# The first mixer of a two-block transformer in another order: latents and values first, attention beside the forget gates, recurrence beside gates and half of the output projection

## The chip, the cores and the metric

One core of a Trainium2 chip runs the whole kernel. The metric is the device time of one execution in microseconds; the time given is the median of three runs. The engines are TensorE (PE in the profile), VectorE (DVE), ScalarE (ACT), GpSimd (POOL) and SyncE (SP), which issues nearly all transfers here.

## What is computed

Two transformer blocks on 256 tokens of width 2048, all in float32. Only the first mixer concerns the change:

```python
mod = (cond @ w_mod[layer] + b_mod[layer])            # six sections of 2048, cond = silu(c)
shift_a, scale_a, gate_a, shift_m, scale_m, gate_m = split(mod)
h = _rmsnorm(x, pre_mix_g[layer]) * (1.0 + scale_a) + shift_a
proj = h @ w_in[layer]                                # 512 + 256 + 64 + 5 * 1024 columns
q_lat, kv_lat, k_rope, hq, f_fwd, f_bwd, hi, hg = jnp.split(proj, offsets, axis=-1)
attn_out = _mla(...)      # rmsnorm of latents, w_uq, w_ukv, rotation, 8 heads, softmax, values
rec_out = _hgrn2_bidir(...)   # two gated recurrences (f_fwd, f_bwd) over values hi, norm, silu(hg)
mix = jnp.concatenate([attn_out, rec_out], axis=-1) @ w_out[layer]
x = x + gate_a * _rmsnorm(mix, post_mix_g[layer])
```

An MLP (w_up, squared relu, w_down) with the sections shift_m, scale_m and gate_m follows, then the second block.

## The kernel before

**Splitting.** Every float32 weight is multiplied as a high part and a low part. A chunk of 512 KB is loaded by SP into one of four slots of w_raw (L594), ScalarE copies it with rounding into w_hi (L1020, L1022), VectorE subtracts and writes w_lo (L1318), TensorE multiplies. "By feature" (L675, L677) the weight is stationary and 256 tokens of high and low activations move past it; "by token" (L701 to L703) the activations are stationary and 512 columns of weights move. A panel is 256 output features of four-tile chunks, or 512 columns of two-tile chunks. It accumulates in one of two pairs of PSUM banks (0 to 3); banks 4 to 7 are for everything else. After a panel ScalarE copies the low sums (half_sum, L1038) and VectorE adds them to the high ones (L1394), or for token panels VectorE writes y (L1440, L1443); TensorE's panel waits until the one two before it is evicted (`summed`).

**Order.** The phases are a list. Each engine has its own instruction queue, written in the order of that list: per panel its splits, then the eviction of the panel before. Work other than projections stands either in a hook ahead of a phase (`before_...`), which runs with no projection between, or in `beside`, after a chunk.

```python
Phase("in_h", 8, [(in_h, 0, 2), (in_h, 1, 2)], Side(2, 2, 8)),
Phase("in_m", 1, [(in_h, 16, 0), (in_h, 17, 0), (in_h, 18, 0), (in_h, 19, 0),
                  (in_m, 0, 0), (in_m, 1, 0), (in_m, 2, 0), (in_r, 0, 0)]),
Phase("uq", 2, [(uq, i, 4) for i in range(4)]),
Phase("ukv", 2, [(ukv, i, 4) for i in range(4)]),
Phase("w_o", 1, [(w_o, i, 0) for i in range(4)], Side(2, 4, 4)),
Phase("up_0", 8, [(up[0], 0, 2), (up[0], 1, 2)], Side(2, 5, 4)),
```

- **in_h**: 16 panels of w_in (queries, both forget gates, half of the values) in a loop. Beside each chunk one piece of w_mod, 512 KB: VectorE multiplies it with silu(c) in two products (`modulation`, L1357, L1360) and adds into mod_acc. `Side(rows, section, pieces)` says which; TensorE adds up the partitions later (`sum_mods`, L818), VectorE takes the result (`take_mods`, L1620).
- **before in_m** (`hgrn_start`): modulation sums, sigmoids of the gates, values transposed to tokens, the diagonal of the recurrence (L853). **in_m**: the last 8 panels (values, output gates, latents). Beside every second chunk one of 14 level steps of the recurrence: 16 products on TensorE (L869), then on VectorE a predicated copy and three multiplications (L1703 to L1716).
- **before uq** (`hgrn_end`): products between the halves (L879), outputs (L887, L888), norm over heads (L895, L900), output gate; and the norms of the latents. It ends with h_lo.
- **uq, ukv**: 8 panels each, of one chunk. The angles of the rotation (`rope_angles`, L1765 to L1776) and the sine (L1240) stand ahead of ukv. SP doesn't load w_out before h_lo.
- **before w_o**: rotation (L928, L1785 to L1800), values transposed, 16 steps of attention (`attention_step`; L934, L935 scores, L773 transposes, L759 values; VectorE L1560 to L1575; ScalarE L1132 to L1146).
- **w_o**: 4 panels by token, 32 chunks, a piece beside each; `squared` and `weighed` prepare the norm.
- **before up_0**: modulation sums, norm, residual (`boundary`, L1468), second norm, transposes (`turn`, L714), activations of the MLP. The same boundary stands behind down_1 (1507 us), without modulation sums.

A hook of VectorE, and all of `beside` for the first panel of a phase, stands ahead of that panel's splits from the fifth on (`follow_stream`).

## Time and profile before

| | us |
|---|---|
| median of 3 runs | 2956.44 (2954.32 to 2957.05) |
| profiled execution | 2949.73 |
| its span | 2947.9 |
| TensorE busy | 2695.3 (91%) |
| VectorE busy | 1908.4 (65%) |
| ScalarE busy | 1205.7 (41%) |
| mean granted clock of TensorE | 0.953 |

The page gives busy time, a chain of work that ended last and the costliest groups. "Granted clock" is the share of full speed that TensorE was allowed (1.00 is 2.4 GHz, 0.5 is 1.2 GHz). The trace can be asked for busy time by window, for groups of instructions, for waits, and for the chain or all instructions in order of time. Times count from the span's start. An arrow names what ended an engine's idle time.

### The profile page before, as it was taken

The page shows a single profiled execution, that of the slowest core. Times are in us where ns is not written, and L with a number is a line of the kernel's source. Part 1 is how long each engine was busy: PE and PEld are TensorE (multiplying, and loading weights), DVE is VectorE, ACT ScalarE, POOL GpSimd, SP SyncE. Part 2 cuts the span into 40 slices and gives each one's busy share as a digit, 9 for nine tenths or more (in the row PEclk, how much of TensorE's full clock was granted, in tenths as well). Part 3 has the DMA queues.
Part 4 walks back from the last instruction along what each step waited for, and adds up shares of the span by engine and source line. Part 5 has one row for each costly group of instructions (what it writes and reads, how often), then busy time and mean ns, then how long its engine had stood idle before and what let it go on. Part 6 is the DMA issues. An engine that isn't in the chain of part 4 may idle for free.

```text
span 2947.9 us, 38886 instructions
## 1 busy us (share of the span) xinstructions
PE 2695.3 (91%) x14139; PEld 2294.5 (78%) x14139; DVE 1908.4 (65%) x2353; ACT 1205.7 (41%) x1532; POOL 22.2 (1%) x41
## 2 busy tenths in 40 slices
PE   1399898689699999999979999999979999999998
PEld 1388897558588888888868888887768888888886
DVE  6799675559688445664554878877556666565444
ACT  2244223334444333444454434455454444444433
POOL 1000000000000000000010000000000000000000
PEclk9699799779799999999989999999989999999999
DMA  9799332319488456665547555554536666665554
GB/s 329 272 386 386 107 115 56 110 50 357 142 286 270 164 189 189 187 188 191 187 124 215 178 171 158 164 165 150 175 120 198 191 186 191 188 188 182 191 186 150
DMA packets 434073, 562.45 MB, mean 191 GB/s; under 512 B 17927, under 2 KB 319427, under 8 KB 433712
## 3 DMA queue, kind: packets, MB, share of 16 engines
q1 hardware_dynamic: 432480, 558.18, 58.0%
q0 software_dynamic: 1488, 2.84, 0.4%
q8 instruction: 69, 1.13, 0.2%
q14 instruction: 36, 0.29, 0.0%
HBM read 558.85 MB, written 2.10 MB: 190 GB/s over the span
## 4 chain that ended last, share of the span: by engine, by line
PE 85%; DVE 7%; DMA 4%; ACT 3%; issue 2%; SPq 0%; DVEq 0%; ACTq 0%
PE ps L675 37%; PE ps L677 18%; PE ps L703 8%; PE ps L701 8%; PE ps L702 8%; DMA w_raw<-in_w_mod 2%; PE ps L869 2%; DVE mod_acc L1360 1%; DVE mod_acc_a L1644 1%; DVE w_lo L1318 1%; PE ps L818 1%; ACT ring L1082 1%; PE ps L721 1%; ACT y L1087 1%; PE ps L759 1%
## 5 line engine op out<-in xcount | busy, mean ns | idle before, releaser
L675 PE MATMUL ps<-acts,w_hi 128*128 128x512 f32 x4464 | 1579.1, 399 | 18.9 <-DVE acts L1488 13.2
L1318 DVE TENSOR_TENSOR w_lo<-w_raw,w_hi 128x1024 fp32r<-128x1024 f32 (+1 forms) x872 | 1054.5, 1213 | 727.5 <-ACT w_hi L1020 376.9
L677 PE MATMUL ps<-acts,w_lo 128*128 128x256 f32 x4464 | 1252.3, 281 | 0.0
L675 PEld LDWEIGHTS ps<-acts,w_hi 128*128 128x128 f32 x4464 | 844.9, 189 | 218.2 <-issue 22.3
L1022 ACT CAST w_hi<-w_raw 128x1024 fp32r<-128x1024 f32 (+2 forms) x592 | 612.7, 1039 | 880.4 <-PE ps L677 698.9
L677 PEld LDWEIGHTS ps<-acts,w_lo 128*128 128x128 f32 x4464 | 848.6, 190 | 2.0 <-issue 1.7
L1020 ACT CAST w_hi<-w_raw 128x1024 fp32r<-128x1024 f32 x280 | 292.9, 1049 | 427.8 <-PE ps L703 376.3
L701 PE MATMUL ps<-w_hi,ff 128*128 128x512 f32 x864 | 341.5, 395 | 0.0
L702 PE MATMUL ps<-w_lo,ff 128*128 128x512 f32 x864 | 341.3, 395 | 0.0
L703 PE MATMUL ps<-w_hi,ff 128*128 128x512 f32 x864 | 341.3, 395 | 0.0
L703 PEld LDWEIGHTS ps<-w_hi,ff 128*128 128x128 f32 x864 | 162.8, 188 | 38.3
L702 PEld LDWEIGHTS ps<-w_lo,ff 128*128 128x128 f32 x864 | 162.8, 188 | 38.1
L701 PEld LDWEIGHTS ps<-w_hi,ff 128*128 128x128 f32 x864 | 162.8, 188 | 38.1
L1360 DVE SCALAR_TENSOR_TENSOR mod_acc<-mod_w,silu_c,mod_acc 128x512 f32<-128x512 f32 x240 | 179.8, 749 | 10.5 <-DMA mod_w<-in_w_mod 4.5
L1038 ACT COPY half_sum<-ps 128x512 f32<-128x512 f32 x168 | 97.2, 579 | 72.7 <-PE ps L677 72.7
L1377 DVE SCALAR_TENSOR_TENSOR pr<-pr,cols (+15 forms) x240 | 114.0, 475 | 10.3 <-DVE pr L1377 5.4
L701 PE MATMUL ps<-w_hi,acts 128*128 128x512 f32 x256 | 100.1, 391 | 1.2 <-DVE w_lo L1318 1.2
L703 PE MATMUL ps<-w_hi,acts 128*128 128x512 f32 x256 | 99.7, 390 | 0.0
L702 PE MATMUL ps<-w_lo,acts 128*128 128x512 f32 x256 | 99.7, 390 | 0.0
L1644 DVE SCALAR_TENSOR_TENSOR mod_acc_a<-w_raw,silu_c,mod_acc_a 128x1024 f32<-128x1024 f32 x60 | 75.9, 1283 | 23.9 <-DMA w_raw<-in_w_mod 22.1
L818 PE MATMUL ps<-ones,mod_acc_a 128*128 128x1 f32 x64 | 13.9, 352 | 82.2 <-DVE mod_acc_a L1644 82.2
L818 PEld LDWEIGHTS ps<-ones,mod_acc_a 128*128 128x128 f32 x64 | 13.8, 332 | 82.5 <-issue 44.2
(250 smaller groups left out, 1677.7 us busy)
## 6 DMA issues: line engine op xcount, KB each, us to landing
w_raw<-in_w_in SPq DMA_DIRECT2D x236, 512.0 KB, 4.1
w_raw<-in_w_down SPq DMA_DIRECT2D x216, 512.0 KB, 3.6
w_raw<-in_w_gate_up SPq DMA_DIRECT2D x176, 512.0 KB, 3.9
mod_w<-in_w_mod SPq DMA_DIRECT2D x128, 512.0 KB, 6.7
w_raw<-in_w_up SPq DMA_DIRECT2D x128, 512.0 KB, 4.3
w_raw<-in_w_mod SPq DMA_DIRECT2D x64, 512.0 KB, 4.9
w_raw<-in_w_out SPq DMA_DIRECT2D x64, 512.0 KB, 5.2
w_raw<-in_w_attn_o SPq DMA_DIRECT2D x16, 512.0 KB, 3.4
```

The costliest lines, as they stand in the source:

```text
L675: pe.matmul(ps[:, bank, :], hi, lin_.act[:, kk, :, :], start=at_first, stop=False, skip_group_check=True)
L677: mm = pe.matmul(ps[:, bank, 0:T], lo, lin_.act[:, kk, 0, :], start=False, stop=at_last, skip_group_check=True)
L701: pe.matmul(o, a_hi, hi, start=at_first, stop=False)
L702: pe.matmul(o, a_hi, lo, start=False, stop=False)
L703: mm = pe.matmul(o, a_lo, hi, start=False, stop=at_last)
L1020: act.copy(wide[1][:, slot, 0:kn, :], wide[0][:, slot, 0:kn, :]).then_inc(hi_ready, 1)
L1022: act.copy(w_hi[:, slot, 0:kn, 0:lin_.width], w_raw[:, slot, 0:kn, 0:lin_.width]).then_inc(hi_ready, 1)
L1038: act.copy(half_sum[:, pair, 0:n, :], ps[:, 2 * pair:2 * pair + n, T:2 * T]).then_inc(half_ready, 1)
L1318: dve.tensor_tensor(low[cut], raw[cut], high[cut].bitcast(F32), ALU.subtract).then_inc(lo_ready, 1)
L1360: ins = dve.scalar_tensor_tensor(acc, w, c, acc, ALU.mult, ALU.add)
L1377: ins = dve.scalar_tensor_tensor(o, z_, w, o, ALU.mult, ALU.add)
L1644: ins = dve.scalar_tensor_tensor(acc, w_mod_slots[:, s, :], c_k, acc, ALU.mult, ALU.add)
```

## The change

The phases of the first mixer are redefined. Latents (in_q, in_kv) and values (l_v) are projected first and by token, so the values need no transposes and the latents are normed by token and then transposed. uq and ukv follow, unrolled. Then 12 panels of forget gates and queries (in_f), with rotation, modulation sums, all attention steps (one per chunk) and the gates' sigmoids beside them. Then the output gates (in_hg, 4 panels) and the attention half of w_out (w_oa, 4 panels of 8 tiles), with the recurrence from its diagonal to its output gate beside them: one level step per chunk. Last the recurrent half of w_out (w_or), added to the first. The recurrence's hooks and attention's hook are gone.

Pieces of w_mod are listed per chunk instead of regular: 26 in in_m and in_v, 6 in uq and ukv, 33 in in_f (from chunk 10), none in in_hg, 10 in w_oa, 21 in w_or; their sum of 96 and the 32 of up_0 are as before. Buffers are laid out anew; x_tok is overwritten and x is loaded again in w_or. `tokens_part` panels are evicted by ScalarE instead of VectorE, in down_0 too. In `follow_stream` only the first four chunks' `beside` of a first panel stand in one go. `before_up_0` waits for the pieces and not for the last eviction. What follows up_0 keeps its code.

```diff
+            Phase("in_m", 1, [(in_q, 0, 0), (in_kv, 0, 0)], sides(gate_a[0:12], range(1, 13))),
+            Phase("in_v", 1, [(l_v, 0, 0), (l_v, 1, 0)], sides(gate_a[12:26], range(1, 15))),
+            Phase("uq", 1, [(uq, i, 0) for i in range(HEADS)], sides(gate_a[26:30], (1, 3, 5, 7))),
+            Phase("ukv", 1, [(ukv, i, 0) for i in range(HEADS)], sides(gate_a[30:32], (1, 4))),
+            Phase("in_f", 1, [(x, i, 0) for x in (l_f, l_b, l_q) for i in range(4)],
+                  sides(shift_m[0:32] + scale_m[0:1], [*range(10, 42), 47])),
+            Phase("in_hg", 1, [(l_g, i, 0) for i in range(4)]),
+            Phase("w_oa", 1, [(w_oa, i, 0) for i in range(4)], sides(scale_m[1:11], range(6, 16))),
+            Phase("w_or", 1, [(w_or, i, 0) for i in range(4)],
+                  sides(scale_m[11:32], sorted([*range(16), *range(4, 14, 2)]))),
...
             for ph in phases:
-                if ph.name == "w_o":
-                    sp.wait_ge(h_lo, 1)
                 for j in range(ph.n_chunks):
                     chunk(ph, 0, j, True)
...
+                    if ph.name == "w_or" and j == 6:
+                        sp.wait_ge(ho_mm, HEADS)
+                        load_x()
...
+                if ph.name == "in_v":
+                    if j == 4:
+                        turn_latent(range(4))
+                    if j == 7:
+                        turn_latent(range(4, 7))
+                if ph.name == "in_f":
+                    if j < 5:
+                        rotate(j)
+                    if j == 6:
+                        pe.wait_ge(rot_done, 6)
+                        pe.wait_ge(side_products, side_all("ukv"))
+                        sum_mods(mod_acc, 2, 5)
+                    if j == 8:
+                        pe.wait_ge(rot_done, 15)
+                        pe.wait_ge(mods_done, 6)
+                        pe.wait_ge(summed, summed_all("ukv"))
+                        turn_values(att1.v, att1.v_turned)
+                    if j == 10:
+                        pe.wait_ge(*att1.v_moved(4))
+                    if 10 <= j < 10 + ATT_STEPS:
+                        attention_step(att1, scores_1, j - 10)
+                    if j == 43:
+                        pe.wait_ge(side_products, 2 * (ph.piece0 + 32))
+                        sum_mods(mod_acc, 2, 4)
...
+            def hgrn_step(g):
+
+                if g == 1:
+                    diagonal()
+                if g == 4:
+                    pe.wait_ge(diag_moved, 4)
+                    pe.wait_ge(q_done, 2)
+                if 4 <= g < 4 + N_STEPS:
+                    level_step(g - 4)
+                if g == 19:
+                    off_diagonal()
+                if g == 21:
+                    outputs()
+                if g == 23:
+                    sum_heads()
+                if g == 26:
+                    spread_heads()
...
             def before_up_0():
-                pe.wait_ge(summed, summed_all("w_o"))
-                pe.wait_ge(side_products, side_all("w_o"))
+                pe.wait_ge(side_products, side_all("w_or"))
+                pe.wait_ge(*o_1.row_moved(4))
                 sum_mods(mod_acc, 2)
...
+                if kind in ("tokens_raw", "tokens_part"):
+                    cut = slice(p0 * lin_.step, p0 * lin_.step + lin_.width)
+                    o = lin_.out[:, :, cut] if kind == "tokens_raw" else by_tokens[ph.name].y[:, :, cut]
+                    if seq:
+                        act.wait_ge(summed, seq)
+                    act.copy(o, ps[:, bank:bank + 2, 0:lin_.width]).then_inc(summed, 1)
+                    if ph.name == "in_m":
+                        act.wait_ge(summed, seq + 1)
+                        latent_squares(b)
                     return
...
+                if ph.name == "uq" and j in (1, 3, 5):
+                    rope_angles((1, 3, 5).index(j))
+                if ph.name == "in_f":
+                    if 4 <= j < 9:
+                        rope(j - 4)
+                    if j == 9:
+                        take_mods(2, 4, 5)
+                        gate_gain("post_mix_g", 2)
+                    if 13 <= j < 13 + ATT_STEPS:
+                        attention_step(att1, j - 13)
+                    forget_step(j)
+                    if j == 46:
+                        take_mods(2, 6)
...
+                if 7 <= g < 7 + N_STEPS:
+                    level_step(g - 7)
...
             def before_up_0():
+                weigh(o_1, 3)
+                dve.wait_ge(*o_1.weighed(4))
                 take_mods(2, 8)
                 scale_gain("pre_mlp_g", 4)
-                boundary(o_1, t_2, "w_o")
+                dve.wait_ge(x_loads, 64)
+                boundary(o_1, t_2, "w_or")
                 turn_low(t_2)
...
             if first and b == 0:
-                for j in ids:
+                for j in ids[:SLOTS]:
                     beside(ph, it, j, first)
             split(ph, it, b, first, ids[SLOTS:])
```

ScalarE takes its attention step u at chunk 13 + u of in_f like VectorE, the sine in ukv at chunk 2, the sigmoids and the scaling of the gates at chunks 32 to 39 (VectorE did the scaling before), and of the recurrence the copies at g = 4, 22 and 24, the root at 26 and the high parts at 29; VectorE has the gate product at 24, the root at 26, the outputs' products at 29 and the low parts at 30 and 31. g counts the chunks of in_hg and w_oa, 0 to 31.

## Rows read from the trace of the kernel before

**Rows 1.** the page's first part: busy us, share of the span, instructions

```profile
PE 2695.3 (91%) x14139; PEld 2294.5 (78%) x14139; DVE 1908.4 (65%) x2353; ACT 1205.7 (41%) x1532; POOL 22.2 (1%) x41
```

**Rows 2.** table of windows: busy us and (instructions) per engine, granted clock, DMA share, GB/s

```profile
130.00:317.00 187.00, 183.95 (x1025) 159.01 (x1026) 178.58 (x231) 79.04 (x90) 0.00 (x0) 0.98 0.99 353
317.00:360.00 43.00, 36.71 (x171) 35.19 (x172) 21.28 (x30) 10.65 (x14) 0.00 (x0) 0.57 0.05 14
360.00:483.00 123.00, 123.00 (x859) 113.41 (x859) 91.86 (x88) 30.87 (x35) 0.00 (x0) 1.00 0.37 105
483.00:532.00 49.00, 33.88 (x170) 25.82 (x168) 21.60 (x24) 22.34 (x36) 0.55 (x1) 0.82 0.05 14
532.00:555.00 23.00, 22.71 (x114) 19.82 (x115) 11.15 (x15) 7.78 (x13) 0.00 (x0) 0.86 0.34 100
555.00:588.00 33.00, 14.13 (x64) 10.74 (x62) 21.09 (x39) 14.72 (x22) 0.00 (x0) 0.76 0.50 175
588.00:646.00 58.00, 49.44 (x154) 26.79 (x154) 27.76 (x79) 19.47 (x60) 0.00 (x0) 0.72 0.00 1
646.00:741.00 95.00, 92.87 (x417) 77.08 (x416) 82.57 (x101) 38.42 (x49) 0.00 (x0) 0.98 0.86 316
741.00:775.00 34.00, 11.43 (x51) 10.29 (x50) 15.52 (x32) 16.68 (x38) 0.00 (x0) 0.58 0.44 152
...
1780.00:1960.00 180.00, 180.00 (x1029) 157.33 (x1028) 155.35 (x282) 80.77 (x126) 0.00 (x0) 1.00 0.56 170
```

**Rows 3.** chain of waits: start us, us, what; the two boundaries of stages

```profile
129.78 0.77 PE ps L675
...
774.78 0.77 PE ps L675
...
1507.25 0.24 PE ps L703
...
1530.74 0.43 PE ps L675
```

**Rows 4.** TensorE in order of time, end of w_o: start us, us, instruction

```profile
735.71 0.39 PE L701 MATMUL ps<-w_hi,acts 128*128 128x512 f32 x1
...
740.47 0.39 PE L701 MATMUL ps<-w_hi,acts 128*128 128x512 f32 x1
```

**Rows 5.** chain of waits beside level steps of the recurrence

```profile
406.67 3.52 PE ps L869 x32
...
415.80 3.52 PE ps L869 x32
```

**Rows 6.** groups by form, 130 to 1000 us: busy us, mean ns | idle before, releaser

```profile
L1318 DVE TENSOR_TENSOR w_lo<-w_raw,w_hi 128x1024 fp32r<-128x1024 f32 x197 | 238.3, 1220 | 67.3 <-ACT w_hi L1020 36.0 <-ACT w_hi L1022 31.0
...
L1360 DVE SCALAR_TENSOR_TENSOR mod_acc<-mod_w,silu_c,mod_acc 128x512 f32<-128x512 f32 x240 | 179.8, 749 | 10.5 <-DMA mod_w<-in_w_mod 4.5 <-DVE mod_acc L1360 0.3
...
L1703 DVE COPY_PREDICATED a_diag<-masks,ps 128x1024 f32<-128x1024 uint8 x14 | 22.8, 1626 | 22.4 <-PE ps L869 22.4
...
L1575 DVE TENSOR_TENSOR acts<-ps,acts 128x256 fp32r<-128x256 f32 x8 | 3.4, 425 | 9.1 <-ACT acts L1146 9.1
...
L1240 ACT ACT_TABLE_LOAD x1 | 1.3, 1283 | 0.0
```

**Rows 7.** waits, 140 to 310 us: us in total, times, longest

```profile
ACT w_hi L1022 <- DMA w_raw<-in_w_in: 85.7, 52, 6.1
```

**Rows 8.** VectorE in order of time, evictions of every second ukv panel

```profile
570.78 0.69 DVE L1394 TENSOR_TENSOR kv<-ps,half_sum 128x512 f32<-128x512 f32 x1 [0.44 <-ACT half_sum L1038]
...
574.52 0.69 DVE L1394 TENSOR_TENSOR kv<-ps,half_sum 128x512 f32<-128x512 f32 x1 [0.43 <-ACT half_sum L1038]
```

**Rows 9.** chain of waits at the boundary after w_o, the modulation sums

```profile
750.09 7.00 PE ps L818 x32
```

**Rows 10.** chain of waits within attention: value product, first score product

```profile
631.09 0.87 PE ps L759 x4
...
631.96 0.43 PE ps L934 x2
```

746 lines of the change are left out of this document (367 added, 379 removed).

## The prediction

> **What bounds the kernel now.** I read the page first: TensorE is busy for 2695 of 2948 us, 91% [rows 1]. So over most of the span nothing but less TensorE work would help, and the diff takes almost none away. Next I cut the stretch that the diff touches into its stages by the table of windows [rows 2]. Outside the first mixer the dense stages are solid (180.0 of 180 us between 1780 and 1960). The mixer is where TensorE idles or runs at its lower level of 1.2 GHz: 317 to 360 (granted clock 0.57: modulation sums, transposes and the start of the recurrence, one after the other), 483 to 532 (33.9 of 49 us busy: end of the recurrence and latent norms), 555 to 588 (14.1 of 33: angles, small panels, late weights), 588 to 646 (58 us of attention alone at 0.72), and 741 to 775 (11.4 of 34: the boundary). That is 217 us with little projection work in them. The reader should see that these stages are serial chains between three engines, not work that fills one.
>
> The third view is the chain of waits. Within it the first projection matmul starts at 129.78 and the first one of w_up at 774.78 [rows 3]. All the diff's effect lies between, 645.0 us, so I cost the new order from the same start to the same end.
>
> **Unit prices.** A weight chunk of 512 KB costs TensorE 2.72 us by token: 21 matmuls lie between two starts at 735.71 and 740.47, 0.227 us each, 12 a chunk [rows 4]. By feature it costs 2.80: two level steps start 9.13 us apart, one of them lasts 3.52, and two chunks lie between [rows 5]. VectorE pays 1.22 us for a chunk's low part and 0.75 for each of the two products of a modulation piece [rows 6]; started one behind the other these overlap, so chunk plus piece plus its share of the eviction is 2.7, and the 64 of each between 130 and 317 come to 173 us. There TensorE, VectorE (179 of 187 busy) and the DMA engines (353 GB/s, share 0.99) are all full [rows 2], and ScalarE waited 85.7 us for weights to land [rows 7]: any new stage with one piece per chunk can't run faster than that pace.
>
> **Part 1, latents and values first, by token (in_m, in_v).** in_q is 8 chunks, 21.8 us; in_kv is 320 columns wide instead of 512, so a matmul is 0.147 and the 8 chunks 14.1; the values, 16 chunks, 43.5. Added: 14 small transposes for the latents, 1.6. The values need no transposes any more. The first token chunk may start after two activation tiles instead of four, about 128, but still at the lower clock: 4 us of loss. 26 of the pieces lie here, so VectorE (28 later splits, 26 pieces, the latent steps: 66 us) and DMA (24 MB still to come at about 137, 68 us at the 353 GB/s of that stage) stay just under TensorE's 74 from there; I take 4 us of joins. The new latent norm sits at the head of in_v: ScalarE evicts, squares, loads a table (1.28, [rows 6]), scales, in about 8 us, and what is queued behind it is the split of chunk 4, which TensorE wants after four chunks, 10.9 us: hidden with 1 to 2 us to spare. Sum 89, ends at 217.
>
> In a sentence apart: the Trainium skill (ScalarE: Activation LUTs, What ACT_TABLE_LOAD costs) gives a switch 1.28 us for the load and 1.38 for a drain; the trace agrees on the first and shows no separate drain. By the page the sum would be at most 3 us longer, for the two loads that lie in a chain (here and the sine).
>
> **Part 2, uq and ukv.** Nothing goes but the wait for w_out's first chunks: SP no longer waits for h_lo there. These are panels of a single chunk, so eviction and the next split alternate on VectorE: ukv now runs two panels in 3.74 us [rows 8] where TensorE needs 2.8. The change lays 6 pieces and the 19 angle operations (6.9 us together, hidden in 555 to 588 of before) between them. Followed panel by panel: uq 27 us (22.4 of TensorE, plus gaps of 1, 2 and 2 us behind the pieces with angles), ukv 15 (8 panels at 1.87, less the first), its two pieces and the sine hidden or not: 0 to 4 us. I take 42 together: ends at 259. The bounds are 37 and 50.
>
> **Part 3, in_f: attention beside forget gates and queries.** 48 chunks at 2.75 are 132. Added on TensorE, at the full clock: rotations 4; two modulation sums of 16, 3.5 each (32 records took 7.0 at the lower clock, [rows 9]); value transposes 2; attention, 0.87 for a value product per two steps and twice 0.43 for the scores of each [rows 10], with the transposes 1.5, times 16 is 24. Sum 37. VectorE per chunk there: split 1.13, piece 1.4, eviction 0.15, attention 1.1 or, with the 1.1 of wait for ScalarE's high part in every other step (9.1 us in 8, [rows 6]) and the low part itself, 2.6: mean 4.5, against TensorE's 2.8 + 1.5 = 4.3. So attention goes at VectorE's pace, 16 x 0.2 = 3, and joins cost some 5: 8 in all. The waits put before the steps (TensorE at chunk j needs VectorE at chunk j+2) leave 8.5 us for a round of 5.8, so I charge nothing for the round trip. The sigmoids move to chunks 33 to 39 of ScalarE, 17.6 us of work in 19.2. Sum 177, ends at 436. What it replaces: 588 to 646, and 317 to 331.
>
> **Part 4, in_hg and w_oa: one level step per chunk instead of one per two.** in_hg: 16 x 2.75 + diagonal 3.5 + 12 x 3.6 = 91. VectorE: the first four copies take 2.45 instead of 1.26 (the mean over 14 is 1.63, [rows 6]), so those steps come to 7.0 with the split against TensorE's 6.4; the three chunks of distance absorb these 2.5 us. The diagonal's two products of 2048 (2.3 each) stand before split 5, and TensorE has 8 us of chunks to cover them. Ends at 527. w_oa: 16 x 2.72 = 43.5, two level steps 7, off-diagonal 3.5 and outputs 7 (16 and 32 products, at a level step's price for 16), sums and spread over heads 7 (16 products of 256 columns at 0.43) = 68. The end of the recurrence (VectorE at chunks 26 to 31: root, gate products 4.9, low parts 2.4, with a piece in each chunk) now has the last chunks of w_oa to hide in; following the queues the split of chunk 31 comes 1 to 2 us late. 70, ends at 597. If that cover fails the cost is the former serial tail, about 15 us.
>
> **Part 5, w_or.** TensorE needs 43.5 + 3.5. VectorE has 16 splits (18), 21 pieces (29), four additions and three weighings of 1.2 (8.5): 55.6. DMA has 17 MB left when it starts, with the reloaded x, 48 us. So VectorE bounds it: 55, ends at 652. This is slower per chunk than w_o now (95 us for 32 chunks and 32 pieces, [rows 2]); the pieces that attention's stage had no room for land here.
>
> **Part 6, boundary.** Before, TensorE's 7.0 us of modulation sums waited for the last eviction, and VectorE's residual for them [rows 9]. Now they wait for the pieces only, beside the last splits. That is the order of the other additive boundary, 1507.25 to 1530.74, 23.5 us [rows 3], plus 2.5 for late w_up chunks and the shift: 26 in place of 34. First w_up matmul at 678.
>
> **The sum.** 774.8 - 678.5 = 96 us less. The profiled execution took 2949.7 (span 2947.9), so it would be 2853.5; the median of runs stands 6.7 above it, so I forecast 2860. down_0's evictions move to ScalarE (4 copies, off the path): nothing.
>
> **Rivals.**
> A. *VectorE bounds the whole mixer.* Its 471 us of work between 130 and 775 [rows 2] now has some 550 instead of 645. If each split waits for the step ahead of it: attention 11 us more, w_oa's tail 6, w_or at w_o's pace of 2.97 per piece 7, early levels and uq 6: 30 more, 2890. For it: w_o shows this pace. Against: TensorE stayed at 123.0 of 123 beside level steps.
> B. *The clock falls in uq and ukv.* The stage table shows 0.86 and 0.76 there. If all of it ran at 1.2 GHz, 33 us of multiplying becomes 60 (its gaps swallowed): some 20 to 25 more, 2883. Against: the low figures begin with idle TensorE (483 to 532, 555 to 565), which the change removes. Beside it: the Trainium skill (TensorE: Matmul & The Clock Gate, A second HAM failure mode) says short idles between groups of matmuls can make the clock swing; by that rule this rival is the outcome.
> C. *Slower than before: TensorE's queue stops at every step laid beside it.* It runs in order, so a step whose operand is late stops the projection too, and then no slot is freed for the next chunks. 16 attention steps, 14 level steps and some 10 others carry such waits. At 2.4 us each the 96 us are gone; at one VectorE round of 3.7 (split, piece, eviction) the loss is 148 and the time 3008. For it: the density has doubled (one per chunk; per two or three before). Against: both present stages with steps between chunks are free of idle time [rows 2].
> D. *Nothing comes of it*, because time saved is given back at w_or and the boundary: that takes A and twice B's price and the old serial tail, about 2945.
> E. *Better than the sum:* uq and ukv without gaps (-5), joins free (-12), w_or at DMA's 48 (-7): 2836.
>
> **How the numbers follow.** Forecast within 2845 to 2878: 0.60. A: 0.17. B: 0.06. E: 0.12. C: 0.03. D: 0.02, of which half is within 0.2%. About 0.2% is what a measurement of this kernel can tell from no change. The range must leave out C and D and the far halves of A and E: 2832 to 2900. Faster 0.96, same 0.01, slower 0.03.
>
> **What would show it.** The first w_up matmul near 678; TensorE over 95% busy at a clock of 1.00 from 260 to 595; level steps 6.3 to 6.4 us apart in in_hg; VectorE over 95% busy in w_or and 55 us for it; gaps of 2 us in uq; 24 to 28 us of boundary. Wrong if level or attention steps lie over 1 us further apart than these, if the clock shows 0.5 between 217 and 259, or if anything behind the boundary moves by more than 3 us.

## The result, and the profile after

The changed kernel takes 2908.15 us (median of 4 runs, 2905.36 to 2916.35), the kernel before 2956.74 beside it (4 runs, 2954.32 to 2958.67). The ratio is 0.9848, with a 95% interval of 0.9823 to 0.9873: 1.5% faster, 48.6 us. I had forecast 2860 and at most 2900. The direction was right, and half of the gain is missing.

The profiled execution has a span of 2903.5 us. First the page's first part: busy us, share of the span, instructions. TensorE's busy time fell by 31 us against [rows 1] and VectorE's by 18; ScalarE's rose by 5.

```profile
PE 2664.2 (92%) x14029; PEld 2264.1 (78%) x14029; DVE 1890.5 (65%) x2331; ACT 1211.0 (42%) x1552; POOL 22.3 (1%) x41
```

The table of windows of the changed kernel, cut where TensorE starts the first matmul of a stage: in_m with in_v, uq with ukv, in_f, in_hg, w_oa, w_or up to the start of its last matmul, boundary. Columns as in [rows 2].

```profile
130.20:217.40 87.20, 84.11 (x398) 70.89 (x399) 77.10 (x116) 41.86 (x64) 0.00 (x0) 0.98 0.85 299
217.40:262.50 45.10, 36.17 (x194) 29.12 (x192) 37.05 (x63) 23.06 (x36) 0.00 (x0) 1.00 0.55 171
262.50:454.00 191.50, 184.49 (x986) 149.43 (x987) 144.84 (x225) 86.75 (x143) 0.00 (x0) 0.97 0.75 229
454.00:555.20 101.20, 94.45 (x675) 88.64 (x673) 77.25 (x68) 22.08 (x26) 0.00 (x0) 0.94 0.35 106
555.20:628.10 72.90, 72.90 (x385) 59.84 (x386) 52.62 (x56) 30.67 (x35) 0.00 (x0) 0.96 0.51 171
628.10:692.40 64.30, 51.74 (x225) 41.44 (x223) 51.82 (x61) 19.54 (x28) 0.00 (x0) 0.92 0.89 313
692.40:720.60 28.20, 7.77 (x50) 6.86 (x48) 19.77 (x35) 19.52 (x44) 0.00 (x0) 0.59 0.39 130
```

What to see: the long serial stretches of [rows 2] (483 to 532, 555 to 588, 588 to 646) are gone, and no stage shows VectorE full: 144.84 of 191.50, 77.25 of 101.20, 51.82 of 64.30. TensorE still idles 7 us in each of in_f and in_hg and 12.6 in w_or. The chain of waits ends the mixer 54.1 us earlier than in [rows 3]; I had forecast 96:

```profile
720.64 0.77 PE ps L655
```

By stage, in us, forecast and measured from first matmul to first matmul:

| stage | forecast | measured | difference |
|---|---|---|---|
| start to in_v's end | ends 217 | 217.4 | 0.4 |
| uq, ukv | 42 | 45.1 | 3 |
| in_f | 177 | 191.5 | 14.5 |
| in_hg | 91 | 101.2 | 10 |
| w_oa | 70 | 72.9 | 3 |
| w_or | 55 | 64.3 | 9 |
| boundary | 26 | 28.2 | 2 |

The sum of the differences is 42 us. Behind the boundary, in code that the change doesn't touch, another 10 us of the gain are gone: 2173.2 us from the first w_up matmul to the end before, 2182.9 after. How the loss divides belongs to this pair of executions: in a second pair (experiment 12) the mixer is 40.7 us shorter, not 54.1, and the part behind it 1.4 us shorter, not 10 longer. The spans differ by 44.4 and 42.1 us.

**Where TensorE stops.** Two views name the waits. In the waits of 533 to 560 us (us in total, times, longest):

```profile
DVE w_lo L1376 <- ACT w_hi L1033: 8.8, 2, 5.2
...
PE ps L917 <- DVE hb L1819: 6.8, 1, 6.8
```

and the table of windows shows the clock at 1.2 GHz from 2.3 us into that stop (it begins at 541.6) to 9 us behind it:

```profile
543.90:557.50 13.60, 9.19 (x38) 8.71 (x39) 10.03 (x12) 0.00 (x0) 0.00 (x0) 0.50 0.24 78
```

TensorE stands once for 6.8 us before a level step, for VectorE's update (L1819). VectorE had not been working: in order of time (start, us, instruction, in brackets the idle time before it) it ran splits of w_oa and stood between them for ScalarE.

```profile
530.37 2.35 DVE L1376 TENSOR_TENSOR w_lo<-w_raw,w_hi 128x1024 fp32r<-128x1024 f32 x2
536.34 1.22 DVE L1376 TENSOR_TENSOR w_lo<-w_raw,w_hi 128x1024 fp32r<-128x1024 f32 x1 [3.62 <-ACT w_hi L1033]
542.73 1.23 DVE L1376 TENSOR_TENSOR w_lo<-w_raw,w_hi 128x1024 fp32r<-128x1024 f32 x1 [5.16 <-ACT w_hi L1033]
543.87 0.68 DVE L1468 TENSOR_TENSOR hg<-ps,half_sum 128x512 f32<-128x512 f32 x1
544.47 1.22 DVE L1806 COPY_PREDICATED a_diag<-masks,ps 128x1024 f32<-128x1024 uint8 x1
```

These are the four first splits of a new phase. The code that orders VectorE and ScalarE (`follow_stream`) does them all, then the eviction, and only then what belongs beside chunks 0 to 3. The fourth split needs a slot that in_hg's last chunk frees. TensorE does what is beside a chunk at once, so it comes to a level step whose update stands in VectorE's queue behind that fourth split.

In w_or the waits (629 to 693 us) are for weights:

```profile
ACT w_hi L1033 <- DMA w_raw<-in_w_out: 30.0, 9, 9.5
ACT ring L1086 <- DVE y L1508: 16.2, 3, 7.0
PE ps L682 <- DVE w_lo L1376: 12.6, 5, 5.2
```

SP's queue in order of time tells why they come late. L577 is a weight load, L587 a modulation piece, L543 x:

```profile
626.89 0.37 SPq L577 DMA_DIRECT2D w_raw<-in_w_out  x1
632.16 2.01 SPq L587 DMA_DIRECT2D mod_w<-in_w_mod  x2
634.22 0.47 SPq L577 DMA_DIRECT2D w_raw<-in_w_out  x1
...
637.09 2.95 SPq L587 DMA_DIRECT2D mod_w<-in_w_mod  x2
640.09 1.16 SPq L543 DMA_DIRECT2D x_tok<-in_x  x2
641.29 0.45 SPq L577 DMA_DIRECT2D w_raw<-in_w_out  x1
```

Between 627 and 632 SP issues nothing: the next load in its queue is a piece, whose slot is freed by a piece that VectorE, by the same rule of four splits first, takes up only at 630.60.

In attention's stage nothing stands still for long, but a chunk takes 5.0, 5.3 or 5.8 us. VectorE and ScalarE in order of time, one chunk each:

```profile
335.03 1.23 DVE L1376 TENSOR_TENSOR w_lo<-w_raw,w_hi 128x1024 fp32r<-128x1024 f32 x1 [1.38 <-ACT w_hi L1036]
336.17 1.53 DVE L1434 SCALAR_TENSOR_TENSOR mod_acc<-mod_w,silu_c,mod_acc 128x512 f32<-128x512 f32 x2
337.62 0.42 DVE L1629 TENSOR_REDUCE small<-ps 128x1 f32<-128x256 f32 x1
338.07 0.15 DVE L1631 TENSOR_SCALAR small<-small 128x1 f32<-128x1 f32 x1
```

```profile
338.26 0.47 ACT L1175 ACTIVATE prob<-ps,small 128x256 f32<-128x256 f32 x1 [3.27 <-DVE small L1631]
338.63 0.19 ACT L1175 ACTIVATION_READ_ACCUMULATOR prob<-ps,small 128x1 f32 x1
338.73 0.36 ACT L1184 COPY prob_t<-ps 128x256 f32<-128x256 f32 x1
338.98 0.39 ACT L1189 CAST att_out<-ps 128x256 fp32r<-128x256 f32 x1
339.24 0.61 ACT L1052 COPY half_sum<-ps 128x512 f32<-128x512 f32 x1
339.72 1.08 ACT L1036 CAST w_hi<-w_raw 128x1024 fp32r<-128x1024 f32 x1
```

TensorE's waits from 262.5 to 454 us show what that does to it. Each of its six stops beside attention ends with ScalarE's copy behind the exponential:

```profile
PE ps L748 <- ACT prob_t L1184: 7.0, 6, 1.9
```

It is one ring through both engines: low part (335.03), piece, maximum, then ScalarE's exponential (338.26, after 3.27 us of idle time), its copies, the high part of the next chunk (339.72), and only then VectorE's next low part, at 340.83.

### The profile page after: what moved, and what is told of

It reads as the page before. It is cut to its first block, busy times and chain, and to the rows that moved or that the text cites. A ratio compares the mean times of both kernels' runs of the same rounds, so it can differ in the third digit from the quotient of the medians.

```text
span 2903.5 us, 38030 instructions
## 1 busy us (share of the span) xinstructions
PE 2664.2 (92%) x14029; PEld 2264.1 (78%) x14029; DVE 1890.5 (65%) x2331; ACT 1211.0 (42%) x1552; POOL 22.3 (1%) x41
## 4 chain that ended last, share of the span: by engine, by line
PE 82%; DVE 8%; DMA 4%; ACT 4%; issue 2%; SPq 0%; DVEq 0%; ACTq 0%
PE ps L655 33%; PE ps L657 17%; PE ps L684 9%; PE ps L683 9%; PE ps L682 9%; DMA w_raw<-in_w_mod 2%; DVE mod_acc L1434 2%; PE ps L917 2%; DMA w_raw<-in_w_in 1%; DVE w_lo L1376 1%; DVE mod_acc_a L1713 1%; ACT w_hi L1036 1%; ACT ring L1136 1%; PE ps L702 1%; DMA w_raw<-in_w_out 0%
## 5 line engine op out<-in xcount | busy, mean ns | idle before, releaser
L1376 DVE TENSOR_TENSOR w_lo<-w_raw,w_hi 128x1024 fp32r<-128x1024 f32 (+2 forms) x872 | 1052.7, 1212 | 779.7 <-ACT w_hi L1033 414.9
L655 PE MATMUL ps<-acts,w_hi 128*128 128x512 f32 x4224 | 1502.5, 399 | 14.3 <-DVE w_lo L1376 7.0
L657 PE MATMUL ps<-acts,w_lo 128*128 128x256 f32 x4224 | 1188.3, 281 | 0.0
L655 PEld LDWEIGHTS ps<-acts,w_hi 128*128 128x128 f32 x4224 | 798.2, 189 | 206.1 <-issue 17.2
L1036 ACT CAST w_hi<-w_raw 128x1024 fp32r<-128x1024 f32 (+2 forms) x560 | 580.5, 1042 | 712.5 <-PE ps L657 660.9
L657 PEld LDWEIGHTS ps<-acts,w_lo 128*128 128x128 f32 x4224 | 804.0, 190 | 2.2 <-issue 1.7
L1033 ACT CAST w_hi<-w_raw 128x1024 fp32r<-128x1024 f32 (+1 forms) x312 | 323.4, 1039 | 554.8 <-PE ps L684 404.4
L684 PEld LDWEIGHTS ps<-w_hi,ff 128*128 128x128 f32 x864 | 162.2, 188 | 37.5
L682 PE MATMUL ps<-w_hi,acts 128*128 128x512 f32 (+1 forms) x320 | 125.6, 393 | 23.3 <-DVE w_lo L1376 15.7
L684 PE MATMUL ps<-w_hi,acts 128*128 128x512 f32 (+1 forms) x320 | 124.1, 388 | 0.0
L683 PE MATMUL ps<-w_lo,acts 128*128 128x512 f32 (+1 forms) x320 | 124.1, 388 | 0.0
L1052 ACT COPY half_sum<-ps 128x512 f32<-128x512 f32 x160 | 93.0, 581 | 64.9 <-PE ps L657 64.9
L682 PEld LDWEIGHTS ps<-w_hi,acts 128*128 128x128 f32 x320 | 61.5, 192 | 38.2 <-issue 13.6
```

Source lines behind the costliest of these rows:

```text
L655: pe.matmul(ps[:, bank, :], hi, lin_.act[:, kk, :, :], start=at_first, stop=False, skip_group_check=True)
L657: mm = pe.matmul(ps[:, bank, 0:T], lo, lin_.act[:, kk, 0, :], start=False, stop=at_last, skip_group_check=True)
L682: pe.matmul(o, a_hi, hi, start=at_first, stop=False)
L683: pe.matmul(o, a_hi, lo, start=False, stop=False)
L684: mm = pe.matmul(o, a_lo, hi, start=False, stop=at_last)
L1033: act.copy(wide[1][:, slot, 0:kn, 0:lin_.width], wide[0][:, slot, 0:kn, 0:lin_.width]).then_inc(hi_ready, 1)
```

## The experiments

Each edit is on the changed kernel unless it says otherwise. All stages are measured like the table above. A single profiled execution has a total that wanders by some 10 us (see below), so the single edits are judged by their stage, and the whole time only where four executions or more were timed. In the executions whose edits don't reach a stage, uq with ukv is 45.0 to 45.2 us, in_hg 101.1 to 101.3 and in_f, in ten of them, 191.0 to 194.9 (mean 193.1). w_oa wanders there from 72.8 to 74.4, w_or from 64.1 to 65.2 and the boundary from 27.1 to 28.3. The expectations of the first runs cut uq with ukv and in_f at the last eviction instead (50 and 189 us where the table has 45.1 and 191.5).

| kernel | uq, ukv | in_f | in_hg | w_oa | w_or | boundary | behind |
|---|---|---|---|---|---|---|---|
| after | 45.1 | 191.5 | 101.1 | 73.0 | 64.3 | 28.2 | 2182.9 |
| levels at once | 45.2 | 194.6 | 90.9 | 71.9 | 64.1 | 28.1 | 2180.3 |
| exponential later | 45.1 | 184.0 | 101.2 | 73.4 | 64.4 | 28.3 | 2192.4 |
| angles later | 41.4 | 193.0 | 101.1 | 74.3 | 64.9 | 27.1 | 2181.6 |
| w_or's order | 45.2 | 191.0 | 101.2 | 73.0 | 60.7 | 28.3 | 2176.3 |
| x early | 45.2 | 194.9 | 101.2 | 74.3 | 59.0 | 28.3 | 2183.0 |
| eviction early | 45.0 | 193.8 | 101.1 | 73.3 | 65.4 | 24.4 | 2179.3 |
| pieces moved | 45.0 | 191.5 | 101.1 | 74.3 | 54.8 | 28.2 | 2180.2 |
| order and x | 45.2 | 192.2 | 101.1 | 74.4 | 55.2 | 28.3 | 2182.7 |
| all seven | 41.5 | 184.1 | 91.0 | 70.7 | 53.1 | 25.3 | 2183.2 |
| all seven, region moved | 41.4 | 182.4 | 91.1 | 71.2 | 53.6 | 24.4 | 2170.1 |

**1. Levels at once.**

```diff
-                    if not (first and b == 0 and j < SLOTS):
+                    if not (first and b == 0 and j < SLOTS) or ph.name in AT_ONCE:
                         beside(ph, it, j, first)
...
-            if first and b == 0:
+            if first and b == 0 and ph.name not in AT_ONCE:
                 for j in ids[:SLOTS]:
```

with `AT_ONCE = ("w_oa",)`, for VectorE and ScalarE.

> Edit: in w_oa VectorE and ScalarE do what belongs beside chunks 0 to 3 behind each chunk's split, and not after all four splits and the eviction. My theory: the 6.75 us in which TensorE stands before a level step at 541.6, and the 1.2 GHz of 544 to 557.5 that follows, come from that order alone (VectorE's step for chunk 0 stands behind the split of chunk 3, which needs in_hg's last chunk used, and TensorE is held before it). Then no gap above 1 us between 535 and 560, clock 1.00 there, in_hg and w_oa together 161 instead of 173 us, first w_up matmul at 708 to 711 instead of 720.6, time about 2897. Rival: VectorE's pace of level steps (6.9 us each with a split) is the cause; then over half of the gap stays and w_up starts at 717 or later. On the pitch of the pairs of matmuls in up_0 and up_1 (346.7 ns before, 353.3 after): if the order of the instructions fixes it, these four runs all show 353.3; if it is settled anew in each execution, some show 346.7.

in_hg fell from 101.1 to 90.9 us and w_oa by 1.1: 11.3 together. In the table of windows there is no idle time and no fall of the clock left:

```profile
530.00:545.00 15.00, 15.00 (x114) 14.12 (x114) 11.67 (x12) 2.10 (x2) 0.00 (x0) 1.00 0.30 99
545.00:558.00 13.00, 13.00 (x93) 12.00 (x92) 10.03 (x12) 2.58 (x3) 0.00 (x0) 1.00 0.37 118
```

The first w_up matmul came at 714.1, not 708 to 711: the execution started uq 2 us later and in_f took 3 more, which the edit doesn't reach. In its stage the theory holds. Of the 11.3 us, 6.75 are the idle time; the rest goes with the low clock (9.2 us of work at half the clock cost 4.6). The rival, VectorE's pace, is out: with 21.7 of 28 us busy it keeps up with one level step per chunk.

**2. Exponential later.**

```diff
-                    if 13 <= j < 13 + ATT_STEPS:
-                        attention_step(att1, j - 13)
+                    if 14 <= j < 14 + ATT_STEPS:
+                        attention_step(att1, j - 14)
```

in ScalarE's part alone.

> Edit: ScalarE's attention step stands one chunk later, behind the high part of the next chunk. My theory: the pace of 5.3 us per attention step (4.5 forecast) is a chain through both engines: VectorE low part, piece, maximum, then ScalarE exponential, copy, high part of the next chunk, then VectorE's next low part. With the high part ahead of the exponential the pace falls to 4.3 to 4.6, in_f ends at 441 to 446 instead of 456.5, w_up starts at 706 to 711, time about 2895. Rival A of the prediction (VectorE's own work is the bound): VectorE is then above 95% busy between 333 and 390 and the pace stays at 5.0 or more. Second rival, the memory for scores and probabilities (two of each) makes the round: the gaps of TensorE before the transposes grow and the pace stays.

in_f took 184.0 us, 7 less than the lowest of the ten others and 9.1 less than their mean. A chunk with an attention step takes 4.5 us on average (from 340.6 to 381.4 in 9), as expected. The stage as a whole gained less than expected: 7.5 us against the first profile, where an end at 441 to 446 would have been 10 to 15. TensorE has no idle time left there, and VectorE is at 84%:

```profile
338.00:386.00 48.00, 48.00 (x252) 37.61 (x251) 40.35 (x84) 21.64 (x49) 0.00 (x0) 1.00 0.76 226
```

So the ring through both engines was the limit; with it cut, TensorE is. Rival A (VectorE's own work) is out, and so is the second rival, for TensorE's stops before the transposes are gone. The first w_up matmul came at 718.6 and not at 706 to 711, since this execution started uq 4.8 us later. The whole time, 2912.76, is above the changed kernel's because its part behind the boundary was 2192.4; the section on the hardware comes back to that.

**3. Angles later.**

```diff
-                if ph.name == "uq" and j in (1, 3, 5):
-                    rope_angles((1, 3, 5).index(j))
+                if ph.name == "uq" and j == 1:
+                    rope_angles(0)
                 if ph.name == "in_f":
+                    if j < 2:
+                        rope_angles(j + 1)
```

and the sine from ukv's chunk 2 to in_f's chunk 3.

> Edit: the two long parts of the rotary angles (8 operations, 2.9 us each) move from uq to chunks 0 and 1 of in_f, the sine to its chunk 3. My theory: uq is bound by VectorE's serial work, 7.5 us for two panels of which 3.0 are angles; then a pair of panels takes 5.6 to 6.0, uq and ukv together 44 to 46 us instead of 50, and in_f loses nothing, for VectorE has room there. w_up starts at 715 to 717, time about 2903. Rival 1: the alternation of eviction and split between the engines sets the panels, and uq stays within 1.5 us of 28.4. Rival 2: the angles come back in in_f, since ScalarE's sine waits for them ahead of the split of chunk 4: gap of over 2 us around 275.

uq with ukv fell to 41.4 us, 3.7 less (4 to 6 expected from 50), all of it in uq (24.1 us, before 27.8), and in_f stayed within its spread, with no stop of TensorE around 275. VectorE's evictions in uq lie at 230.11, 232.89 and 235.94, TensorE's pace, where two panels took 7.5 us. Rival 1 and rival 2 are out. The first w_up matmul came at 721.0 and not at 715 to 717: uq started 1.9 us later, and in_f and w_oa were 1.4 and 1.3 longer, within their spread.

**4. w_or's order.** `AT_ONCE = ("w_or",)`, and for SP

```diff
-                    for piece in pieces_at(ph, j):
+                    late = ph.name == "w_or"
+                    for piece in pieces_at(ph, j - late) + (pieces_at(ph, j) if late and j == 15 else []):
                         side(ph, 0, *piece)
```

> Edit: in w_or alone, pieces of chunks 0 to 3 are worked off behind each split and not after four splits and the eviction, and SP issues a chunk's pieces behind the load of the next chunk. My theory: w_or takes 63.7 us and not 55 because weight loads stand in SP's queue behind loads of pieces that wait for a free slot (chunk 5's load is issued at 634.2, its slot was free at about 628; ScalarE then waits 9.5 us for it). Then chunk 5's load is issued by 630, ScalarE's waits for weights fall from 28 us to under 12, w_or ends 5 to 8 us earlier and w_up starts at 713 to 716, time about 2901. Rival: the reloaded x (2 MB) and the total of bytes are the bound: at 640 to 660 the DMA engines then stay at 380 GB/s or more, the gap of 5.2 us at 651 stays and w_up starts at 718 or later.

Chunk 5's load was issued at 629.95 instead of 634.22, ScalarE's waits for weights fell from 30.0 to 9.3 us and the stop of 5.2 us is gone. Yet w_or took only 3.6 us less, where I expected 5 to 8, and the first w_up matmul came at 717.6, not 713 to 716. The direction is right and the size is not: this is a part of the cause. Of the rival, the DMA rate did come (393 GB/s from 640 to 660).

**5. x early.**

```diff
-                    if ph.name == "w_or" and j == 6:
+                    if ph.name == "w_oa" and j == 14:
                         sp.wait_ge(ho_mm, HEADS)
                         load_x()
```

> Edit: the reload of x (2 MB) is issued behind chunk 14 of w_oa and not behind chunk 6 of w_or. What is asked: how much of w_or's 64.3 us (first to last matmul) is the burst of x in the middle of its weights. Theory 1, the burst holds back the weights behind it (load of chunk 8: 11.4 us from issue to landing): the gap of 5.2 us at 651 shrinks below 2 us, w_or takes 60 to 62. Theory 2, the bound is VectorE's serial work and the order of the queues: w_or stays within 1.5 us of 64.3, and w_oa gets no longer either. Bad case: SP's queue now waits in w_oa for the recurrence's outputs and w_oa gets 1 to 3 us longer.

w_or took 5.3 us less (59.0). w_oa took 74.3, which is within its spread, so the bad case is not shown. The burst of 2 MB in the middle of w_or's weights is the other part.

**6. Order and x together, all 21 pieces left in place.**

> Edits of two earlier runs together, and no piece moved: in w_or pieces behind each split and loads of pieces behind the next chunk's, and x issued in w_oa. What is asked: whether w_or with all 21 pieces can run at what I forecast as VectorE's bound, 55 us (55.6 of work by the rows of before; 51.4 measured as busy). Theory: the excess of 64.3 over 55 was only waits in the queues; then w_or takes 55 to 57 and w_up starts 8 to 9 us earlier by the two edits' sum (3.6 and 5.3). Rival: with 21 pieces VectorE's queue (splits, pieces, additions, weighings and the joins at three panel borders) doesn't go below 58; then only moving the pieces helps (54.8 with 16 of them).

w_or took 55.2 us, 9.1 less, the sum of both (3.6 + 5.3). VectorE is at 90% of it, and ScalarE waits 2.9 us for weights instead of 30.0:

```profile
632.60:687.80 55.20, 49.62 (x225) 40.20 (x224) 49.73 (x59) 19.31 (x28) 0.00 (x0) 0.97 0.93 327
```

So the stage can run in the 55 us that I forecast, and the 9 us above it were waits in the two queues. That VectorE's work is what sets the 55 is not shown: it was busy for 49.7 us, where I had 55.6, and experiment 7 takes away 5 pieces and still needs 54.8.

**7. Pieces moved.**

```diff
-            Phase("in_hg", 1, [(l_g, i, 0) for i in range(4)]),
-            Phase("w_oa", 1, [...], sides(scale_m[1:11], range(6, 16))),
+            Phase("in_hg", 1, [...], sides(scale_m[1:6], (0, 1, 2, 3, 6))),
+            Phase("w_oa", 1, [...], sides(scale_m[6:16], range(6, 16))),
...
-                  sides(scale_m[11:32], sorted([*range(16), *range(4, 14, 2)]))),
+                  sides(scale_m[16:32], range(16))),
```

> Edit: five of w_or's 21 modulation pieces move, by way of w_oa, to chunks 0 to 3 and 6 of in_hg, where VectorE stood idle for 4.0 and 3.7 us and the DMA engines at 101 to 132 GB/s. Theory: w_or is bound by the sum of VectorE's work and of its queue order, so 5 x 1.53 = 7.6 us go from it (60.7 or less where it took 64.3, likely 57 to 58), and in_hg gets at most 2 us longer. Rival A of the prediction in its strong form, VectorE bounds in_hg as well: in_hg gets 5 us or more longer and nothing is won at the first w_up matmul.

w_or took 54.8 us and in_hg the same 101.1: five pieces cost nothing in in_hg and 9.5 us in w_or, more than their 7.6 of VectorE's time and w_or ended below the 57 to 58 that I expected. That each piece also holds up SP's queue would explain it, but it was not tested by itself.

**8. Eviction early.**

```diff
-            split(ph, it, b, first, ids[:SLOTS])
+            early = 2 if b and ph.name == "w_or" else SLOTS
+            split(ph, it, b, first, ids[:early])
...
-            split(ph, it, b, first, ids[SLOTS:])
+            split(ph, it, b, first, ids[early:])
```

> Edit: in w_or, from the second panel on, the finished panel before is evicted (VectorE's addition and weighing, ScalarE's squares) after two splits of the new one and not after four. Theory: at each of the three panel borders ScalarE stands in its queue for VectorE's addition, which stands behind four splits and their pieces (ScalarE waits 5.2 us at 670 to 676, then VectorE 1.4, TensorE 3.4 at 676.6). Then the gaps of 3.4 and of 1.7 us at the borders fall below 1 us and w_or takes 59 to 61 us instead of 64.3. Rival, VectorE is simply full (its work in w_or is 51.4 us of 63.7): the gaps only move and w_or stays at 63 or more.

A miss: w_or took 65.4 us. TensorE's stops moved (2.3, 2.3, 3.2, 0.8 and 3.3 us, 11.9 in all where it was 12.6) and hardly shrank, as the rival said, though not for its reason: VectorE was at 85%, and ScalarE still waited 25.4 us for weights. While loads are late, the order of the evictions is no lever inside w_or. The boundary behind was 3.8 us shorter, so w_or and boundary together took 89.8 us, below the 91.7 to 92.7 of the seven executions that no edit touches there; why, I have not followed up.

**9. All seven edits.**

> All edits of the seven single ones together: levels and pieces behind each split, the exponential one chunk later, angles later, SP's order in w_or, x early, eviction after two splits, five pieces moved. If the causes add up: in_f 8 us less, in_hg and w_oa 11 less, uq 4 less, w_or 8 to 12 less, so from the start of uq to the first w_up matmul 470 us instead of 503, and the median near 2875. If they share a bound (VectorE at over 95% in in_hg or w_or) the gain stays under 22 us, 2886 or more.

2868.32 us (4 runs, 2866.61 to 2872.64), 0.9707 of the kernel before (0.9664 to 0.975). From the start of uq to the first w_up matmul it takes 465.7 us, where the changed kernel takes 503.2: 37.5 less, more than the 33 expected. Across the stages the edits add up: 3.6 us in uq and ukv, 7.4 in in_f, 12.4 in in_hg and w_oa, 11.2 in w_or, 2.9 at the boundary. Inside w_or they do not: order with x gave 9.1 us and the moved pieces 9.5, and all together give 11.2. TensorE is busy for 49.3 of its 53.1 us by then, and VectorE for 47.0.

**10. The place of one tile.** The changed kernel was short of 10 us behind the boundary. I looked for it in the addresses: the change places a new tile of 32 bytes ahead of the large shared region, which moves from 130816 to 130848.

```diff
+        place("pad", [P, 8], F32)
         big = at[0]
```

> Edit: 32 unused bytes are placed ahead of the big region, and nothing else. The change itself put a tile of 32 bytes (lat_root) ahead of it, so every tile in the region, the bias among them, stands 32 bytes further than before. What is asked: why TensorE stands 3.3 to 5.7 us before a matmul of in_c some 33 us behind the second boundary in all nine kernels with the new order and not at all in the kernel before, where the weights beside the load of the bias (runs of 256 bytes) land 13 us after issue and not 8.5. Theory: the loads of the bias write to addresses that are a multiple of 32 but not of 64 and take longer on the DMA engines; then the gap is gone, the DMA rate beside the bias load is near 260 GB/s instead of 187, and the time behind the boundary, without what the pitch of matmul pairs costs, is 4 us shorter (2168 to 2170 instead of 2171 to 2177). Rival: the address has no part in it, the gap stays at 3.3 or more. Nothing ahead of the boundary moves by more than 3 us by either.

The gap in in_c stayed (3.6 us), so the theory as I put it fell. But the part behind the boundary was 2176.3 us. Less the excess of the pitch (summed over all pairs of matmuls by feature, what their distance is above 346.7 ns; see the last section) it was 2168.0, against 2173.7 in the changed kernel: something else had become faster, and the forecast of 2168 to 2170 was met by luck. It is the matmuls by token on the feed-forward tiles. The table of windows for 50 us of down_0 shows 216 of them in the changed kernel and 220 with the padding:

```profile
1000.00:1050.00 50.00, 50.00 (x216) 40.22 (x215) 22.07 (x18) 19.36 (x19) 0.00 (x0) 1.00 0.58 189
```

```profile
1000.00:1050.00 50.00, 50.00 (x220) 41.04 (x219) 22.06 (x18) 19.90 (x20) 0.00 (x0) 1.00 0.58 192
```

In the mean they start 233.3 ns apart with the region at 130848 and 228.9 with it at 130880. down_0 and down_1 are 3.4 us shorter each, down_2 with the end 4.7.

> All edits together, as before (2868 us), and the 32 bytes ahead of the big region. Theory of the address: 4 us less, median 2864 (the pitch of the matmul pairs, which changes from run to run, adds or takes 3). Rival: the same 2868 within 2.

2855.06 us (6 runs, 2850.59 to 2868.59), 0.9662 of the kernel before (0.9638 to 0.9687). Both were wrong: it is 13 us below the version without the padding and not 4 or 0. The profiles put the 13 us behind the boundary (2170.1 against 2183.2), but the two intervals overlap, so the runs alone do not show them. This is the fastest version, 53 us below the changed kernel by the medians.

**11. The kernel before, with its region at 130880.** The same line with `[P, 16]` on the kernel before.

> Edit, on the kernel before the change: 64 unused bytes ahead of the big region (which then starts at 130880 and not at 130816), and nothing else. In the run with 32 bytes added to the changed kernel the matmuls by token on the feed-forward tiles, which lie in that region (also 130880 there, 130848 without), came 228.9 ns apart and not 233.3: 3.4 us less for down_0, 3.4 for down_1 and 4.6 for down_2 and the end. Theory: this is the place of the stationary operand and has nothing to do with the new order; then the kernel before gains the same 10 to 12 us, median of the ratio 0.996, and the pitch in down_0 falls from 233.3 to 229. Rival: it belongs to another tile that the change moved, or to the state of one execution; then the pitch stays at 233 and the ratio within 0.998 to 1.002.

The pitch did what the theory says, 228.9 ns, and 220 matmuls in the same window. The whole time did not follow: 2951.94 us in 12 runs, 2952.86 beside it in 17 of the kernel before, ratio 0.9999 (0.9983 to 1.0015). In its profile up_0, up_1 and gate_up are 3.0, 3.4 and 9.1 us longer than in the first profile of the kernel before, all by the other pitch of matmuls by feature. Whether the two are tied or that was chance stays open. The new place also brings the gap in in_c to the kernel before: 2.7 us, where it had none.

**12. Both kernels once more, unchanged.**

> The changed kernel, unchanged, profiled a second time. If the pitch of the matmul pairs is settled in each execution: at least one of up_0, up_1, in_c and gate_up shows the other of 346.7 and 353.3 ns than in the first profile, and the span behind the first w_up matmul differs from 2182.9 by 3 us or more. If it belongs to the program: the same pitch in each of them and 2182.9 within 1.5. The stages ahead of the boundary (48.0, 95.6, 64.3) repeat within 1 us by both, in_f within 3 (three or two short falls of the clock).

> The kernel before, unchanged, profiled a second time. If the gap in in_c belongs to the execution: it is there, 2 to 5 us, some 33 us behind the second boundary, and in_c and the following projections up to the attention take 244 to 248 us, as in the changed kernels, instead of 241.8. If it belongs to the change: no gap, as in the first profile. The first w_up matmul stays within 4 us of 774.8 and the stage ahead of it repeats.

The changed kernel repeats uq (45.2), in_hg (101.1), w_or (65.2) and the stage behind (2181.4). Of its phases, up_0 went from 353.3 to 346.7 ns a pair; up_1 and gate_up kept theirs. The part behind the boundary moved by 1.5 us, where I had said 3 or more, and in_f by 3.1, just over my 3. The kernel before shows the other pitch in in_h, up_1 and gate_up: its first w_up matmul came at 768.4 instead of 774.8, outside of my 4 us, and the rest took 2182.7 instead of 2173.2. So 6 us ahead of the boundary and 10 behind it belong to the execution, and a single pair of profiles can't tell where a gain of that size was lost. Its gap in in_c is again absent (0.1 us).

**13. The region back in its place.**

```diff
-        lat_root = place("lat_root", [P, 2, 2], F32)
+        lat_root = place("lat_root", [P, 2, 2], F32, at[0])
```

It shares the bytes of a tile that is used later, so the region starts at 130816 again.

> Edit: on the changed kernel lat_root takes the address of y_sums, which is used later, so that the big region starts at 130816 again, as in the kernel before, and not at 130848. What is asked: whether the gap in in_c and the slower landing of the bias (median 8.3 and 9.0 us in the changed kernel, 8.3 in the old one moved by 64 bytes, against 6.9 and 7.1 in the old one as it is) come from that place. Theory, by those six rows: a run of 256 bytes that starts on a multiple of 256 is written faster than one that straddles it; then the bias lands after 7 us, the gap is below 0.5 us, the time behind the first w_up matmul, less the excess of the pitch, is 2168 to 2170. Rival: the new order brings the gap with it (another alignment in time of the weights and the bias loads); then it stays at 3 us or more with a landing of 8 or more. The matmuls by token on the feed-forward tiles stay at 233 ns by both.

The gap fell to 1.3 us, between the theory's 0.5 and the rival's 3. The load of the bias, whose runs are 256 bytes, lands as fast as in the kernel before again. From the view of that load's line, us from issue to landing, first the changed kernel, then this one:

```profile
DMA to landing us min/median/max: 3.3/8.3/10.5
```

```profile
DMA to landing us min/median/max: 2.9/7.2/7.7
```

With the region at 130816, a multiple of 256, the median is 6.9, 7.1 and 7.2 us (both kernels); elsewhere it is 7.6 to 9.0 in fourteen profiles. The matmuls by token did not stay at 233 ns but came at 232.4. Behind the boundary, less the pitch, it takes 2167.8 us instead of 2173.7 and 2175.3; the kernel before takes 2167.9 and 2164.6. All eleven profiles with the region at 130848, whose code behind the boundary is the same, lie between 2169 and 2177 (mean 2174). So the 32 bytes cost some 6 us of the change's gain; how many exactly, one profile can't tell. The Trainium skill (DMA: Bandwidth & Descriptors, How a descriptor splits into AXI transactions) says that a transaction may read less than 256 bytes but must start from a multiple of 256, and that the first one of a descriptor that starts elsewhere begins at the multiple below. By that account a piece of 256 bytes that starts elsewhere takes two. The landings agree with it, though these pieces are written there and the page speaks of reads; no row shows the transactions themselves.

## Why the prediction was right and wrong, step by step

- **What bounds the kernel.** Right. The serial stretches of [rows 2] are gone, and the mixer is 54 us shorter in the first pair of profiles, 41 in the second.
- **Part 1.** Right: 217.4 against 217 (up to 222.2 in the fourteen profiles of the new order).
- **Part 2.** 45.1 against 42, within its bounds. uq was priced right, 27.8 against 27, with gaps of 1.1, 1.6 and 1.6 us where I had 1, 2 and 2. ukv took 17.3 against 15: the term for its pieces and the sine, which I had bounded by 0 and 4 and taken at 0, was 2.3. Two panels of uq take 7.5 us where an angle part stands between them, since eviction, split, piece and angles stand one behind the other on VectorE; experiment 3 took 3.7 us of it away.
- **Part 3.** The step that failed in the waits is "I charge nothing for the round trip". I looked at the distance in chunks between TensorE and VectorE; TensorE never stopped for VectorE's part of a step, only for ScalarE's. I did not follow the ring between VectorE and ScalarE: the exponential waits for this chunk's maximum, and in ScalarE's queue the next high part stands behind it. I had charged the wait for the high part in every other step, and it was there in every step (1.38 us in one, 0.26 or 0.52 in the next, beside 0.71 for att_out): 5.3 us a chunk instead of 4.5. Cutting the ring took 7.5 us off the stage, 9 against the mean. That is not 7.5 of the 14.5 that were missing, though, for I had charged 8 us for VectorE's pace and the joins, and all idle time of TensorE in the stage is 7.0 us: that sum was about right by luck. What the sum of 177 left out is TensorE's. Work laid beside the chunks took 41 to 42 us where I had 37, of it attention 27.4 where I had 24. The falls of the clock to 1.2 GHz, two or three of 3.4 or 6.8 us, cost 5.1 us here (10.2 us at half the clock), and I had none. And most projection chunks cost 2.83 us (pairs 353.3 ns apart) where I had 2.75, some 4 us in 48 chunks.
- **Part 4.** The price of the work was right: with experiment 1 in_hg takes 90.9 against 91 and w_oa 71.9 against 70. What failed is the order at the border of two phases, for which the sum of 91 has no term. I followed each queue inside a phase and did not ask in which order it starts the next one, though what VectorE does beside a chunk and when was the matter of the whole diff. The level steps inside in_hg lie 6.35 us apart (ScalarE's splits at 484.44, 490.79 and 497.14), as forecast.
- **Part 5.** 64.3 against 55. "So VectorE bounds it" was the wrong reason for a price that the stage can reach: VectorE was 81% busy, with 51.8 us of work where I had 55.6. I had written down SP's load of x and the bytes, and not which loads stand behind which waits in SP's queue. Experiments 4, 5 and 6 give 3.6 and 5.3 us, and 55.2 together.
- **Part 6.** 28.2 against 26.
- **Behind the boundary.** I had put it down at nothing, and named a move of over 3 us as a sign of error. It moved by 10 in the first pair of profiles and by -1 in the second. Less the excess of the pitch it is 6 and 11 longer; some 6 of that is the place of the region (experiment 13); the rest stays open.
- **Rivals.** A named the time nearest (2890 against 2908) and the wrong cause. B is out: the granted clock is 1.00 through all of uq and ukv, with eleven idle times of 0.1 to 1.6 us between panels. The rule of the Trainium skill (TensorE: Matmul & The Clock Gate, A second HAM failure mode), by which short idles between groups of matmuls can make the clock swing, did not act in uq and ukv. C had its mechanism right at seven places of some forty: TensorE's queue stopped once for 6.75 us and six times for 0.2 to 1.9 us, 13.8 in all, against the 96 or more that it needed.
- **The range.** Its upper end, 2900, left room for 40 us of misses. The seven stages alone missed by 42, all to the same side. In two of the three large ones one omission lies behind it: I priced the work and did not follow the queues round (in_hg, w_or). The third, in_f, is TensorE work and clock that the sum had too small.

With the waits in the queues removed the kernel comes near the forecast stage by stage, 41.4, 182.4, 91.1, 71.2, 53.6 and 24.4 us against 42, 177, 91, 70, 55 and 26. Its median is 2855 us against 2860. That agreement is partly luck: with the region left at 130848 it is 2868, and this version has five pieces moved out of w_or and an eviction order that the forecast kernel did not have. The rows of in_f and in_hg:

```profile
260.00:442.40 182.40, 182.35 (x986) 148.30 (x987) 149.90 (x241) 90.28 (x145) 0.00 (x0) 0.98 0.80 252
442.40:533.50 91.10, 91.10 (x674) 85.39 (x673) 81.77 (x76) 22.08 (x26) 0.00 (x0) 1.00 0.34 101
```

## What to carry to other kernels

A sum of prices tells what a stage can take, and the orders of the queues tell what it takes: for each step laid beside a stream, follow the ring of engines until it comes back to the first, and ask what stands behind the waiting instruction in each queue, the one that issues loads too. Look at the borders of phases by themselves, since prologues there put work in another order than inside. And when tiles are placed by hand, a new small one belongs behind the large regions: 32 bytes cost some 6 us here.
